# Conv taps and the last gate panels spread over the second attention's steps, and the last residual products and norms by token halves

## The reference

```
hx = modulate(rms_norm(x, norm1_g), sh1, sc1)
q, k, v, u, g = split(hx @ w_in)                 # 8 heads of 128, 2 key heads
attn = softmax(q k^T / sqrt(128)) v              # 512 queries, 768 keys (256 of a context)
y_a  = attn @ w_attn_out
h    = depthwise_conv(a * sigmoid(b)), 31 taps, 512 channels     # u = a, b
y_b  = silu(layer_norm(h)) @ w_conv_out
x    = x + g1 * ((sigmoid(g_a) * y_a + sigmoid(g_b) * y_b) @ w_out)
h2   = modulate(rms_norm(x, norm2_g), sh2, sc2)
x    = x + g2 * ((gelu(conv3(h2 @ w_up_a)) * (h2 @ w_up_b)) @ w_down)
out  = rms_norm(x, final_g)
```

## Time and profile before

| | us |
|---|---|
| median of 3 runs | 1760.67 (1759.32 to 1760.96) |
| the profiled execution | 1761.15 |
| its span, first to last instruction | 1759.4 |
| TensorE busy with matmuls | 1651.0 |
| VectorE busy | 1115.5 |
| ScalarE busy | 722.5 |
| mean granted clock | 0.975 |

### The profile page before, as it was taken

How to read it: one execution, slowest core, us unless ns; L and a number is a source line. 1 busy time by engine, 2 the same in 40 slices (tenths; PEclk the granted TensorE clock), 3 DMA queues, 4 the chain that set the end, 5 groups by cost and what they waited for, 6 DMA issues and landing times.

```text
span 1759.4 us, 21542 instructions
## 1 busy us (share of the span) xinstructions
PE 1651.0 (94%) x7712; PEld 1339.7 (76%) x7712; DVE 1115.5 (63%) x1722; ACT 722.5 (41%) x1220; POOL 165.3 (9%) x187
## 2 busy tenths in 40 slices
PE   7979889998999999999989999998799799999996
PEld 5867666666887888888867788887577588888885
DVE  6465588886666665753578478888665644444455
ACT  5234685665443132322443244445433443233232
POOL 0001310000030000000001980000000000000000
PEclk9989899998999999999999999999899899999998
DMA  4226751110354555442313221222233133322332
GB/s 155 96 81 190 161 113 49 49 60 27 108 227 166 172 194 206 161 167 72 95 44 126 94 68 48 62 59 61 64 122 96 60 95 96 96 95 95 96 96 95
DMA packets 48669, 185.37 MB, mean 105 GB/s; under 512 B 6784, under 2 KB 7040, under 8 KB 46160
## 3 DMA queue, kind: packets, MB, share of 16 engines
q1 hardware_dynamic: 38304, 136.75, 24.1%
q0 software_dynamic: 10288, 47.60, 9.3%
HBM read 172.23 MB, written 6.85 MB: 102 GB/s over the span
## 4 chain that ended last, share of the span: by engine, by line
PE 74%; DVE 11%; ACT 2%; issue 2%; DMA 0%; ACTq 0%; DVEq 0%; SPq 0%
PE ps L1839 18%; PE ps L1841 18%; PE ps L1840 18%; PE ps L2209 2%; PE ps L2210 2%; PE ps L2211 2%; PE ps L2043 1%; PE ps L2045 1%; PE ps L2044 1%; PE ps L2004 1%; PE ps L2265 1%; DVE w_lo L1133 1%; DVE conv L1700 1%; PE ps L2029 1%; PE ps L1984 1%
## 5 line engine op out<-in xcount | busy, mean ns | idle before, releaser
L1839 PE MATMUL ps<-h_hi,w_hi 128*128 128x512 f32 x1088 | 436.0, 401 | 38.9 <-DVE w_lo L1156 13.0
L1841 PE MATMUL ps<-h_hi,w_lo 128*128 128x512 f32 x1088 | 427.5, 393 | 0.0
L1840 PE MATMUL ps<-h_lo,w_hi 128*128 128x512 f32 x1088 | 427.5, 393 | 0.0
L1839 PEld LDWEIGHTS ps<-h_hi,w_hi 128*128 128x128 f32 x1088 | 206.7, 190 | 94.7 <-DVE w_lo L1156 13.0
L1133 DVE TENSOR_TENSOR w_lo<-raw,w_hi 128x1024 fp32r<-128x1024 f32 x167 | 210.3, 1262 | 100.3 <-ACT w_hi L613 81.1
L1840 PEld LDWEIGHTS ps<-h_lo,w_hi 128*128 128x128 f32 x1088 | 207.2, 190 | 43.7 <-issue 2.2
L1841 PEld LDWEIGHTS ps<-h_hi,w_lo 128*128 128x128 f32 x1088 | 206.6, 190 | 43.7
L567 ACT ACTIVATE w_hi<-raw 128x1024 fp32r<-128x1024 f32 x131 | 137.7, 1052 | 170.1 <-DMA raw<-in_panels 163.8
L1839 PE MATMUL ps<-f_hi,w_hi 128*128 128x512 f32 x432 | 176.2, 408 | 0.0
L1841 PE MATMUL ps<-f_hi,w_lo 128*128 128x512 f32 x432 | 170.7, 395 | 0.0
L1840 PE MATMUL ps<-f_lo,w_hi 128*128 128x512 f32 x432 | 170.4, 394 | 0.0
(11 more groups left out here) (398 smaller groups left out, 2842.6 us busy)
## 6 DMA issues: line engine op xcount, KB each, us to landing
raw<-in_panels SPq DMA_DIRECT2D x252, 512.0 KB, 3.5
wm<-in_w_mod POOLq DMA_DIRECT2D x16, 1536.0 KB, 7.9
scratch_r<-r POOLq DMA_DIRECT2D x8, 320.0 KB, 9.1
X<-in_x SPq DMA_DIRECT2D x4, 512.0 KB, 7.5
bias<-scratch_c POOLq DMA_DIRECT2D x8, 256.0 KB, 8.4
kd<-k_hi POOLq DMA_DIRECT2D x16, 128.0 KB, 3.7
kd<-k_lo POOLq DMA_DIRECT2D x16, 128.0 KB, 5.3
bias<-scratch_r POOLq DMA_DIRECT2D x8, 256.0 KB, 3.0
```

The costliest lines, as they stand in the source:

```text
L1839: pe.matmul(out, w_hi[:, u, b, :], hi[:, k, :N], start=start, stop=False)
L1840: pe.matmul(out, w_hi[:, u, b, :], lo[:, k, :N], start=False, stop=False)
L1841: ins = pe.matmul(out, w_lo[:, u, b, :], hi[:, k, :N], start=False, stop=stop)
```

## The change

**Taps.** Five taps go to a new place ahead of step 0, before the wait for the root of q_r and its reciprocal; step 0 has 7 (it had 8); steps 1 to 12 have 1, 2, 1, 2 (they had 1, 1, 1, 2); steps 13 to 16 have 1, 1, 0, 1 (13 and 14 had 5, 15 and 16 had 9 each). The sum stays 96.

**Gate panels.** Panels 1 to 13 stay where they are, in steps 0 to 12 (panel 1 in one run). Panel 14 is spread over steps 13 and 14, panel 15 over steps 15 and 16, four blocks a step. Panel 14 is read out in ScalarE's step 15 and panel 15 in its step 17. TensorE's wait for all gate banks ahead of attn_out is dropped (the panel's own waits stay).

**Halves.** out2 and down_2 do panels 0 to 3 as before. Panels 4 to 7 go to banks 0 to 3, first all four for tokens 0 to 255, then all four for tokens 256 to 511. The sum of squares, its column sum, root and reciprocal and the norm's tiles are made for each half, those of the first while TensorE is at the second half. up_0's panels 0 to 3 are done in the same way (`half_panel`), in banks 0 to 3, and their read-out (`up` with a bank) stands ahead of the loop over the rest. The stores of the result are 16 of half a tile.

```diff
-    TAPS_AT = {(0, 1): 8, (15, 0): 1, (15, 1): 2, (15, 2): 2, (15, 3): 4, (16, 0): 2, (16, 2): 2, (16, 3): 5}
-    for w in range(1, 15):
-        for n, count in enumerate((1, 1, 1, 2)):
+    TAPS_AT = {(-1, 0): 5, (0, 1): 7}
+    for w in range(1, 17):
+        for n, count in enumerate((1, 2, 1, 2) if w < 13 else (1, 1, 0, 1)):
             TAPS_AT[w, n] = count
+    GATE2_RUN = {0: (1, 0, (8, 0, 0, 0, 0))}
+    for w in range(1, 13):
+        GATE2_RUN[w] = (w + 1, 0, (1, 1, 1, 2, 3))
+    for w in range(13, 17):
+        GATE2_RUN[w] = (14 + (w - 13) // 2, 4 * ((w - 13) % 2), (1, 1, 1, 1, 0))
+    GATE2_OUT = {g: g for g in range(14)}
+    GATE2_OUT.update({15: 14, 17: 15})
...
-        for f in range(KT):
-            sp.wait_ge(sem("final2_tile"), f + 1)
-            sp.dma_start(out[:, f, :], X[:, f, :]).then_inc(sem("out_stored"), 16)
+        for half, c in enumerate(TOKENS):
+            for f in range(KT):
+                sp.wait_ge(sem("final2_tile"), KT * half + f + 1)
+                sp.dma_start(out[:, f, c], X[:, f, c]).then_inc(sem("out_stored"), 16)
...
 # ScalarE
+        first_squares("out2", "norm_ffn")
+        root("norm_ffn", 0)
+        ffn_high(0, 0)
+        ffn_high(0, 1)
+        second_square("out2", "norm_ffn", 4)
+        ffn_high(0, 2)
+        ffn_high(0, 3)
+        panel_hi(BASE["up_0"])
+        second_square("out2", "norm_ffn", 5)
+        ffn_high(0, 4)
+        ffn_high(0, 5)
+        ffn_high(0, 6)
+        second_square("out2", "norm_ffn", 6)
+        panel_hi(BASE["up_0"] + 1)
+        ffn_high(0, 7)
+        second_square("out2", "norm_ffn", 7)
+        panel_hi(BASE["up_0"] + 2)
+        root("norm_ffn", 1)
+        panel_hi(BASE["up_0"] + 3)
+        for f in range(KT):
+            ffn_high(1, f)
...
 # VectorE
-        dve.wait_ge(sem("q_rms"), 1)
-        chain(dve.reciprocal(q_r[:], q_r[:]))
...
+        taps_at(-1, 0)
+        dve.wait_ge(sem("q_rms"), 1)
+        chain(dve.reciprocal(q_r[:], q_r[:]))
         for w in range(UNITS + 2):
...
+        first_sums("out2", "norm_ffn", 16)
+        inverse("norm_ffn", 0)
+        ffn_value(0, 0)
+        ffn_value(0, 1)
+        second_add("out2", 4, 16)
+        ffn_low(0, 0)
+        ffn_value(0, 2)
+        ffn_low(0, 1)
+        ffn_value(0, 3)
+        square_sum("norm_ffn", 8, TOKENS[1])
+        ffn_low(0, 2)
+        ffn_value(0, 4)
+        second_add("out2", 5, 16)
+        ffn_low(0, 3)
+        ffn_value(0, 5)
+        panel_lo(BASE["up_0"])
+        ffn_low(0, 4)
+        ffn_value(0, 6)
+        square_sum("norm_ffn", 9, TOKENS[1])
+        ffn_low(0, 5)
+        ffn_value(0, 7)
+        second_add("out2", 6, 16)
+        ffn_low(0, 6)
+        ffn_low(0, 7)
+        square_sum("norm_ffn", 10, TOKENS[1])
+        second_add("out2", 7, 16)
+        panel_lo(BASE["up_0"] + 1)
+        square_sum("norm_ffn", 11, TOKENS[1])
+        inverse("norm_ffn", 1)
+        ffn_value(1, 0)
+        ffn_value(1, 1)
+        ffn_low(1, 0)
+        panel_lo(BASE["up_0"] + 2)
+        for f in range(1, KT):
+            if f == 4:
+                panel_lo(BASE["up_0"] + 3)
+            ffn_value(1, f + 1) if f + 1 < KT else None
+            ffn_low(1, f)
...
+        first_sums("down_2", "final2", 40)
+        inverse("final2", 0)
+        for m in range(4, 8):
+            final_tile(0, 2 * m - 8)
+            final_tile(0, 2 * m - 7)
+            second_add("down_2", m, 40)
+            square_sum("final2", m + 4, TOKENS[1])
+        inverse("final2", 1)
+        for f in range(KT):
+            final_tile(1, f)
...
 # TensorE
+        def by_halves(group, name, ready, hi, lo, blocks):
+
+            for m in range(4):
+                panel(0, m, group, ps[:, m % 2, :], blocks, hi, lo, ready=ready)
+            for m in range(4, 8):
+                pe.wait_ge(bank_free, BASE[group] + HALF_FREE[m])
+                half_panel(BASE[group] + m, m - 4, 0, hi, lo, blocks, ready if m == 4 else None).then_inc(sem("half_out"), 1)
+            for m in range(4, 8):
+                pe.wait_ge(sem("half_added"), HALF_BASE[group] + m - 3)
+                half_panel(BASE[group] + m, m - 4, 1, hi, lo, blocks,
+                           at_four=(lambda: half_sum(name, 0)) if m == 4 else None).then_inc(used, 1)
...
+        by_halves("out2", "norm_ffn", lambda k: (bank_free, BASE["conv_out"] + k // 2 + 1 + 2), h_hi, h_lo, ALL)
+        for m in range(4):
+            pe.wait_ge(bank_free, BASE["up_0"] + m - 1)
+            half_panel(BASE["up_0"] + m, m, 0, ready=(lambda k: (n_lo, 24 + k + 1)) if m == 0 else None)
+            half_sum("norm_ffn", 1) if m == 0 else None
+        for m in range(4):
+            half_panel(BASE["up_0"] + m, m, 1, ready=(lambda k: (n_lo, 32 + k + 1)) if m == 0 else None).then_inc(used, 1)
```

More of the change, by code:

```diff
@@ L1040, in up @@
                        .then_inc(sem("hidden_hi"), 1)
[L1041 removed]
+            if c == 0:
+                for u in range(RING):
+                    up(0, u, u >= AHEAD, u)
+            loop(act, g, up, start=c == 0)
             if c < 2:
                 only_split(f"down_{c}")
[L1044 to L1045 removed]
+        first_squares("down_2", "final2")
+        root("final2", 0)
+        for m in range(4, 8):
+            second_square("down_2", "final2", m)
+        root("final2", 1)
     @block.vector
@@ new lines, in first_sums @@
+        def first_sums(group, name, gain):
+            for m in range(8):
+                if m < 6:
+                    panel_lo(BASE[group] + m + AHEAD)
+                if m < 4:
+                    dve.wait_ge(used, done(BASE[group] + m))
+                    x_plus(m % 2, m, slice(0, T), gain).then_inc(bank_free, 1)
+                else:
+                    dve.wait_ge(sem("half_out"), HALF_BASE[group] + m - 3)
+                    x_plus(m - 4, m, TOKENS[0], gain).then_inc(sem("half_added"), 1)
+                if m:
+                    square_sum(name, m - 1, slice(0, T) if m <= 4 else TOKENS[0])
+            square_sum(name, 7, TOKENS[0])
@@ new lines, in second_add, with inverse, ffn_value @@
+        def second_add(group, m, gain):
+            dve.wait_ge(used, done(BASE[group] + m))
+            x_plus(m - 4, m, TOKENS[1], gain).then_inc(bank_free, 1)
+        def inverse(name, half):
+            dve.wait_ge(n_rms, SUMS[name] + half + 1)
+            chain(dve.reciprocal(rstd[:, TOKENS[half]], rstd[:, TOKENS[half]]))
+        def ffn_value(half, f):
+            c = TOKENS[half]
+            dve.wait_ge(n_lo, 24 + 8 * half + f - 1) if f >= 2 else None
+            dve.scalar_tensor_tensor(tmp_v[:, f % 2, c], X[:, f, c], gains[:, 16 + f:17 + f], rstd[:, c], ALU.mult, ALU.mult)               .then_inc(n_val, 1)
@@ L2213, in gate2_fill, with gate2_run @@
                 ins.then_inc(used, 1)
-        def gate2_run(w, first, count):
-            if w < 15:
-                for k in range(first, first + count):
-                    gate2_fill(w + 1, k)
+        def gate2_run(w, n):
+            if w in GATE2_RUN:
+                g, at, counts = GATE2_RUN[w]
+                for k in range(at + sum(counts[:n]), at + sum(counts[:n + 1])):
+                    gate2_fill(g, k)
         for m in range(H2 + 1):
```

191 lines of the change are left out of this document (104 added, 87 removed).

## The result

The changed kernel takes **1747.55 us** (median of 6 runs, 1745.36 to 1748.78) where the kernel before takes 1760.82 (6 runs): a ratio of 0.993, with a 95% interval of 0.9918 to 0.9941. That is 13.3 us. The two profiled executions differ by 13.4 us (1759.4 and 1746.0), so the difference can be looked up stretch by stretch.

What follows compares the result with a forecast made beforehand. TensorE, busy 1651.0 of 1759.4 us, bounds the kernel; time is only where it waits or runs slow. Taps and gates 3.5, out2/up_0 halves 3.5 and down_2 halves 1.4 give 8.4 us: 1752.2, 8 in 10 within 1746 to 1757.6.

Steps and rivals of the forecast that it cites:

- Start: Before step 0 of the second attention: first row maxima 2.3 us later, TensorE's wait for gate panel 2 1.5 later.
- Steps 1 to 12: Second attention: a sixth tap costs nothing in even steps, some 0.25 us in five odd ones, 1.2 us in all.
- Steps 13 to 16: End of second attention: 2.0 us back from steps 13 and 14; TensorE resumes in step 16 at about 1235.3.
- The sum: LayerNorm column sum in attn_out: at 1249.2 instead of 1252.3, 3.1 us earlier, with ScalarE late next instead of taps.
- The clock behind the sum: Stretch 1241.8 to 1258.0, granted clock 0.79: only 0.4 us of the loss at 1.2 GHz taken back.
- Part B: out2, norm_ffn and first up_0 panels in token halves: 3.5 us gained, bounds 0 and 6.5.
- H: End of the fourth first half of out2, put at 1354.4; the walk's times there count from it.
- Part C: down_2 and the end in halves: 1.4 us gained, bounds 0.3 and 2.7.
- More falls at new waits: Rival: three uncovered clock falls at the new waits, 1.6 us each; gain 3.6, 1757.1 us; 16%.
- Waits vanish: Rival: VectorE and ScalarE run ahead of the walk; gain 14.5 us, 1746.2; 18%.
- The ring or ScalarE swallowing A and B: Rival: ring slots or ScalarE's chain leave taps-and-gates and out2/up_0 halves 1 us each; gain 3, 1757.7 us; 10%.
- Slower by the sixth tap: Rival: VectorE sets all 12 steps, each 0.78 us longer, 9.4 in all, plus clock falls; 1768 us; 6%.

Runs made afterwards that it cites:

- the gates alone: The kernel before with the moved gate panels alone, the taps staying where they were: 1759.46 us, ratio 0.9995.

## Why the prediction was right or wrong

The direction, the range for 8 in 10 and most of the walk were right. The forecast missed 4.9 us of gain. By the stretches of the table, gains measured and said are -1.4 and -2.3 ahead of F, +0.9 and -0.4 to step 13, 2.6 and 2.0 to step 15, 4.3 and 3.8 to S, 2.5 and 0.4 to O, 4.5 and 4.9 to the end. The two stretches in which the clock had fallen, F to step 13 and S to O, make 3.4 of it. Another 0.7 is no gain of the change: it lies ahead of the last q_lo.

- **Start, right but for what it covered.** F was to come 2.3 us later. It came 1.4 later in the pair of traces, but 2.1 later counted from the last q_lo ahead of the taps. (The prediction's "1 us free" doesn't give its 2.3; VectorE's idle time there was 0.91 + 0.73, and 3.9 less 1.6 does.) TensorE waited 1.23 us for gate panel 2, as before. What I had not allowed for is that the fall of the clock that stands there in the trace of before need not be in another execution: 1.2 us in this comparison. That part of the gain in the traces is chance as far as the runs show, since the gates alone lack the fall too.
- **Steps 1 to 12, right.** The sum for F to step 13 was 1.2 of odd steps less 0.8 of the shorter row of taps, +0.4. Against the kernel with the gates alone, which has no fall there either, it is 145.0 to 144.64, +0.4. The odd steps 3 to 11 are each 0.25 us longer and step 0 is 0.8 shorter (10.51 for 11.30), both as walked.
- **Steps 13 to 16, a little low.** Steps 13 to 15 gave 2.6, not 2.0, and only where both edits were there, since the bound is TensorE's in one and VectorE's in the other. TensorE resumed at 1232.5 instead of 1235.3, behind the ScalarE copies as said; counted from step 15's row maximum that is 11.2 us, which is the walk's own number.
- **The sum, right.** From step 15's row maximum to S the walk had 25.1 us (1224.1 to 1249.2); it took 24.6.
- **The clock behind the sum, too low: this is the term that was mis-sized.** I took back 0.4 of the loss at 1.2 GHz behind S, because TensorE would still wait about 2 us there at once. It waited 1.4, and the whole of the loss behind S came back: S to O is 2.5 us shorter, and 64.4 to 64.6 in every kernel whose wait for the sum is 1.8 or less. With the 1.2 of the start that makes 3.7 us of clock where the forecast had 0.4. The Trainium skill (TensorE: Matmul & The Clock Gate, HAM oscillation) says that a TensorE that waits between bursts pays for the fall each time. The four traces with a wait of 2.6 us agree; those at 1066, and the last column sum, show that a fall can also stay away behind the same wait.
- **Part B, right.** It was to give 3.5; O to the fifth up_0 panel shortened by 3.6. Shifted by the start of out2, the first reciprocal ended where the walk had it (H+4.5), the last first-half low at H+16.3 (H+16.4 said), the splits of up_0+2 and +3 at H+24.7 and H+28.5 (24.2 and 27.9), and the fifth panel started at H+44.3 (43.8). TensorE's waits from 1290 to 1400 are listed below. The second column sum, w_lo of two panels and the output whose bank the fifth panel needs were named; the 1.3 for the last h_lo of the first half follows from VectorE's one wait; the 1.5 stands at out2's start and was there before (1.48).

```profile
PE ps L1997 <- DVE sq_acc L1451: 1.6, 1, 1.6
PE ps L1967 <- DVE h_lo L1870: 1.5, 1, 1.5
PE ps L1989 <- DVE h_lo L1493: 1.3, 1, 1.3
PE ps L1989 <- DVE w_lo L1160: 1.0, 2, 0.7
PE ps L1967 <- DVEq L1926: 1.0, 1, 1.0
```

- **Part C, a little high.** 1.4 said, 1.0 in the pair of traces, 0.8 to 1.3 like against like. I had charged ScalarE's square between addition and sum, and had not asked whether the order was the best one. Two sums of the prediction are off: the terms of the tail add to 1757.9 and not 1758.0, and with 0.33 us for a half the last eight tiles would be done 0.7 us sooner than the 3.3 that it counts, not 1.2. Neither bears on the forecast.
- **The rivals.** More falls at new waits: wrong, they became fewer in Part A. Waits vanish: its total, 14.5, is near what came, but VectorE and ScalarE did not run ahead of the walk; the clock did. The ring or ScalarE swallowing A and B: wrong. Slower by the sixth tap: wrong, F to step 13 grew by 0.4 in all, not by 9.4, and the even steps stayed as long as they were.

What stays open: why the fall near 1066 and the one in the last column sum come in some traces and not in others, with the same instructions and the same waits ahead of them. Open too is whether the length of the wait is what brings the fall behind the LayerNorm sum: fourteen traces of fourteen go by it there, and moving five taps switched it, but elsewhere a wait of 3.75 us was followed by full clock.
